# Hybrid encoder layer: local kernels of the state-space branch built on four 32-column strips, readout turns every second slot

## The reference

```python
def windowed_gqa_sink(q, k, v, sink):        # |t-s| <= 128, 8 heads, 2 kv heads, blocks of 128 queries
    scores = einsum(q, k) * HEAD_DIM ** -0.5 - slopes * dist      # + a sink logit per head
    probs = softmax(concat([scores, sink_logit]))[..., :-1]
    out = einsum(probs, v)

def s5_scan(u, lam, log_dt, b, c):           # per direction; 32 groups of 16 channels, 64 complex states
    lam_bar = exp(lam * dt);  b_bar = ((lam_bar - 1.0) / lam)[..., None] * b
    bu = einsum('blgc,gnc->blgn', u, b_bar)
    xs = associative_scan(lam_bar, bu)
    return einsum('blgn,gcn->blgc', xs, c).real

y = gelu(y_f + y_b + ssm_d * u)
```

## Time and profile before

| | us |
|---|---|
| median of 3 runs (2711.31 to 2716.84) | 2712.11 |
| the profiled execution, whole | 2706.54 |
| its span, first to last instruction | 2704.9 |
| granted clock of TensorE, mean over the span | 0.986 |
| attention stage in it, about | 258 to 477.9 |
| PE busy over the span | 2607.4 (96%) |
| DVE, ACT, POOL busy | 1597.7, 917.4, 827.5 |

### The profile page before, as it was taken

One profiled execution on the slowest core, in us unless ns is written; L12 is line 12 of the kernel. 1 busy time (PEld: TensorE's weight loads), 2 busy tenths in 40 slices (PEclk: granted clock), 3 DMA queues, 4 the chain that ended last, 5 costly groups with the idle time before them and its releaser, 6 DMA issues. The chain is left out here.

```text
span 2704.9 us, 33938 instructions
## 1 busy us (share of the span) xinstructions
PE 2607.4 (96%) x12118; PEld 2118.6 (78%) x12118; DVE 1597.7 (59%) x2050; ACT 917.4 (34%) x1579; POOL 827.5 (31%) x1070
## 2 busy tenths in 40 slices
PE   7999899999999799999999999999999999999997
PEld 6887566788887588878878888878888888887886
DVE  5202785687896274635687776697677762224342
ACT  5221776512211340123443333343333342123221
POOL 2072000387882000012244444434444320001111
PEclk9999999999999899999999999999999999999999
DMA  6484778644427636365434222212222264336653
GB/s 219 139 281 116 158 156 221 210 140 147 153 94 220 181 144 241 144 156 157 139 102 146 87 70 86 86 55 94 86 86 77 80 196 130 107 86 187 180 153 111
DMA packets 386110, 380.21 MB, mean 141 GB/s; under 512 B 52016, under 2 KB 322352, under 8 KB 381744
## 3 DMA queue, kind: packets, MB, share of 16 engines
q1 hardware_dynamic: 327024, 279.71, 35.7%
q10 hardware_dynamic: 49088, 50.91, 5.8%
q0 software_dynamic: 9856, 47.72, 5.2%
...
## 5 line engine op out<-in xcount | busy, mean ns | idle before, releaser
L522 PE MATMUL tl_banks<-gu_b_hi,gu_a_hi 128*128 128x512 f32 x1232 | 482.5, 392 | 13.4 <-DVE gu_b_lo L1760 8.0
L524 PE MATMUL tl_banks<-gu_b_lo,gu_a_hi 128*128 128x512 f32 x1232 | 481.5, 391 | 0.0
L523 PE MATMUL tl_banks<-gu_b_hi,gu_a_lo 128*128 128x512 f32 x1232 | 481.3, 391 | 0.0
L522 PEld LDWEIGHTS tl_banks<-gu_b_hi,gu_a_hi 128*128 128x128 f32 x1232 | 232.7, 189 | 65.0 <-issue 13.4
L146 PE MATMUL tl_banks<-dn_w_hi,dn_f_hi 128*128 128x512 f32 x704 | 274.3, 390 | 3.3 <-DVE dn_w_lo L1932 2.5
L147 PE MATMUL tl_banks<-dn_w_hi,dn_f_lo 128*128 128x512 f32 x704 | 273.9, 389 | 0.0
L148 PE MATMUL tl_banks<-dn_w_lo,dn_f_hi 128*128 128x512 f32 x704 | 273.9, 389 | 0.0
L523 PEld LDWEIGHTS tl_banks<-gu_b_hi,gu_a_lo 128*128 128x128 f32 x1232 | 232.7, 189 | 48.2
L524 PEld LDWEIGHTS tl_banks<-gu_b_lo,gu_a_hi 128*128 128x128 f32 x1232 | 232.4, 189 | 48.5
L1754 DVE TENSOR_TENSOR gu_a_lo<-gu_raw,gu_a_hi 128x512 fp32r<-128x512 f32 x220 | 198.3, 902 | 91.0 <-ACT gu_a_hi L1536 91.0
L1536 ACT ACTIVATE gu_a_hi<-gu_raw 128x512 fp32r<-128x512 f32 x220 | 138.4, 630 | 240.1 <-PE tl_banks L524 213.1
...
## 6 DMA issues: line engine op xcount, KB each, us to landing
...
```

What stands on the lines that cost most here:

```text
L522: pe.matmul(out, w_hi, x_hi, start=first, stop=False, skip_group_check=again)
L523: pe.matmul(out, w_lo, x_hi, start=False, stop=False, skip_group_check=again)
L524: return pe.matmul(out, w_hi, x_lo, start=False, stop=last, skip_group_check=again)
```

## The change

- A build now takes all four strips of 32 columns of the PE array: pair w = 4 j + part goes to the partitions 32 part to 32 part + 31 of `t_psum`. One bank then holds all 16 pairs of a direction. There are four builds instead of eight, each of 16 matmuls instead of 8 (the same 64 in all), two for each direction, at slots 75, 76, 107 and 108. DVE takes the bank away once for each direction, over 128 partitions.
- `kernels` has 128 partitions by 4 x 15 x 16 values instead of 32 by 16 x 15 x 16. `place_local` therefore needs 8 DMAs for each l instead of 2 (64 instead of 16, each a quarter of the size), `d_diag` is loaded by 8 DMAs instead of 2, and its mask takes three POOL additions instead of one.
- `add_diagonal` moves from slot 105 to 110.
- The readout turns move from slots 10, 11, 12, 13 to 10, 12, 14, 16; the turns of the input tables one slot later.
- `turn_share`, `copy_share`, `apply_share` and `store_out` move one slot later in every tile (2, 3, 5, 6 to 3, 4, 6, 7).
- The table code moves into two generators (`into_tables`, `outof_tables`) with a semaphore and a scratch tile for each direction; the 96 instructions stay on DVE in the same order.

```diff
@@ -2377,16 +2378,17 @@
               [outof[1][r][:].rearrange("p q k c -> p (q k c)")[:, 0:table] for r in range(2)]]
     b_table = [[b_flat[d][r].rearrange("p (q l c) -> p q l c", q=QS, l=SSM_L) for r in range(2)] for d in range(2)]
     params, bbar, rising, falling = bases.params, bases.bbar, bases.rising, bases.falling
-    late = m.sb("kernels", [P, QS * SPAN * SSM_CH])
-    kernels = carve(late, {"kernels": (2 * SSM_CH, (QS, SPAN, SSM_CH))})["kernels"]
+    PARTS = 4
+    late = m.sb("kernels", [P, 2 * 2 * 4 * 2 * SSM_N])
+    kernels = carve(late, {"kernels": (P, (QS // PARTS, SPAN, SSM_CH))})["kernels"]
 
     c_rows = carve(late, {"c_rows": (P, (2, 2, 4, 2 * SSM_N))})["c_rows"]
     c_t = m.sb("c_t", [P, 2, 2, QS, SSM_CH])
 
-    d_diag = m.sb("d_diag", [2 * SSM_CH, QS, SSM_CH])
-    d_mask = m.sb("d_mask", [2 * SSM_CH, SSM_CH])
+    d_diag = m.sb("d_diag", [P, QS // PARTS, SSM_CH])
+    d_mask = m.sb("d_mask", [P, 4 * SSM_CH])
     b_pair = m.sb("b_pair", [P, 2, 2, QS, 2, SSM_CH])
-    table_temp = m.sb("table_temp", [P, QS // 4, POWERS, SSM_CH])
+    table_temp = [m.sb(f"table_temp{d}", [P, QS // 4, POWERS, SSM_CH]) for d in range(2)]
 
     neg_scores = m.sb("neg_scores", [P, 2, WIDE])
     probs = m.sb("probs", [P, 2, WIDE])
...
-    PER_BANK = BANK // LC
-    K_BANKS = QS // PER_BANK
+    local_rows = local_scratch.rearrange("p (q a) m -> a p q m", a=2 * PARTS)
 
 
     COLUMNS = [slice(a * QS // 4, (a + 1) * QS // 4) for a in range(4)]
 
-    C_AT = {10 + n: n for n in range(4)}
-    INTO_AT = {**{25 + 2 * n: n for n in range(8)}, **{49 + 2 * n: 8 + n for n in range(8)}}
-    KERNELS_AT = {**{74 + 2 * n: n for n in range(K_BANKS)}, **{97 + 2 * n: K_BANKS + n for n in range(K_BANKS)}}
+    C_AT = {10 + 2 * n: n for n in range(4)}
+    INTO_AT = {**{26 + 2 * n: n for n in range(8)}, **{50 + 2 * n: 8 + n for n in range(8)}}
+    KERNELS_AT = {75: 0, 76: 1, 107: 2, 108: 3}
     PAIR_AT = {24 + n: n for n in range(8)}
-    DIAG_AT = 105
+    DIAG_AT = 110
 
     def keys_of(kind):
...
@@ -2508,10 +2546,10 @@
         def place_local(ls):
             sync.wait_ge(kernels_ready, 1)
             for l in ls:
-                for e in range(2):
-
-                    sync.dma_start(local_rows[l * SSM_CH:(l + 1) * SSM_CH, e],
-                                   kernels[e * SSM_CH:(e + 1) * SSM_CH, :, SSM_L - 1 - l:2 * SSM_L - 1 - l, :]
+                for a in range(2 * PARTS):
+
+                    sync.dma_start(local_rows[a, l * SSM_CH:(l + 1) * SSM_CH],
+                                   kernels[a * SSM_CH:(a + 1) * SSM_CH, :, SSM_L - 1 - l:2 * SSM_L - 1 - l, :]
                                    .rearrange("c q k o -> c q (k o)")).then_inc(local_placed, 16)
 
         load(1)
...
                     sync.dma_start(c_rows[:, d, r, :, twice * SSM_N:(twice + 1) * SSM_N], rows).then_inc(c_loaded, 16)
-        for e in range(2):
-            rows = ssm_d.rearrange("(a q e c) -> e a q c", a=1, e=2, c=SSM_CH)[e]
-            sync.dma_start(d_diag[e * SSM_CH:(e + 1) * SSM_CH], rows.broadcast_to([SSM_CH, QS, SSM_CH]))\
+        for e in range(2 * PARTS):
+            rows = ssm_d.rearrange("(a q e c) -> e a q c", a=1, e=2 * PARTS, c=SSM_CH)[e]
+            sync.dma_start(d_diag[e * SSM_CH:(e + 1) * SSM_CH], rows.broadcast_to([SSM_CH, QS // PARTS, SSM_CH]))\
                 .then_inc(d_loaded, 16)
         for n in range(2):
             load_u(n)
...
@@ -2535,19 +2573,23 @@
                 place_local(range(0, 2))
         place_local(range(2, SSM_L))
         sync.wait_ge(outof_stored, 4 * 16)
-        sync.wait_ge(local_placed, 2 * SSM_L * 16)
+        sync.wait_ge(local_placed, 2 * PARTS * SSM_L * 16)
...
         pool.wait_ge(bias_step, 2 + N_HEADS)
         pool.memset(b_pair[:], 0.0).then_inc(b_pair_zero, 1)
-        pool.wait_ge(d_loaded, 32)
-        pool.tensor_tensor(d_mask[:], ident[0:2 * SSM_CH, 0:SSM_CH], ident[0:2 * SSM_CH, SSM_CH:2 * SSM_CH],
-                           ALU.add).then_inc(d_diag_ready, 1)
-        pool.wait_ge(d_diag_ready, 1)
-        pool.tensor_tensor(d_diag[:], d_diag[:], d_mask[:].rearrange("p (a c) -> p a c", a=1)
-                           .broadcast_to([2 * SSM_CH, QS, SSM_CH]), ALU.mult).then_inc(d_diag_ready, 1)
+        pool.wait_ge(d_loaded, 2 * PARTS * 16)
+        for n, width in enumerate((64, 32, 16)):
+            of = d_mask if n else ident
+            if n:
+                pool.wait_ge(d_diag_ready, n)
+            pool.tensor_tensor(d_mask[:, 0:width], of[:, 0:width], of[:, width:2 * width], ALU.add)\
+                .then_inc(d_diag_ready, 1)
+        pool.wait_ge(d_diag_ready, 3)
+        pool.tensor_tensor(d_diag[:], d_diag[:], d_mask[:, 0:SSM_CH].rearrange("p (a c) -> p a c", a=1)
+                           .broadcast_to([P, QS // PARTS, SSM_CH]), ALU.mult).then_inc(d_diag_ready, 1)
         for b in range(TILES):
             pool.wait_ge(share_ready, b + 1)
...
@@ -2647,23 +2689,24 @@
             turn.then_inc(into_turned, 1)
 
         def make_kernels(n):
-            d, part = n // K_BANKS, n % K_BANKS
+            d, half = n // 2, n % 2
             k0 = 0 if d == 0 else 1
-            if part == 0:
+            if half == 0:
                 pe.wait_ge(outof_ready[d], 1)
-            if n:
-                pe.wait_ge(kernels_copied, n)
-            else:
-                pe.wait_ge(into_copied, 16)
-
-                pe.wait_ge(b_pair_ready, 8)
-            for j in range(PER_BANK):
-                w = part * PER_BANK + j
+                if d:
+                    pe.wait_ge(kernels_copied, 1)
+                else:
+                    pe.wait_ge(into_copied, 16)
+
+                    pe.wait_ge(b_pair_ready, 8)
+            for j in range(2 * half, 2 * half + 2):
                 for r in range(2):
-                    done = pe.matmul(t_psum[0:2 * SSM_CH, j * LC:(j + 1) * LC],
-                                     b_pair[:, d, r, w].rearrange("p e c -> p (e c)"),
-                                     outof[d][r][:, w, k0:k0 + SSM_L].rearrange("p k c -> p (k c)"),
-                                     start=r == 0, stop=r == 1)
+                    for part in range(PARTS):
+                        w = j * PARTS + part
+                        done = pe.matmul(t_psum[part * 2 * SSM_CH:(part + 1) * 2 * SSM_CH, j * LC:(j + 1) * LC],
+                                         b_pair[:, d, r, w].rearrange("p e c -> p (e c)"),
+                                         outof[d][r][:, w, k0:k0 + SSM_L].rearrange("p k c -> p (k c)"),
+                                         start=r == 0, stop=r == 1)
             done.then_inc(kernels_done, 1)
 
         pe.sem_inc(turned, 2)
...
@@ -2680,7 +2723,7 @@
                 turn_probs(b, i)
                 if i % QUAD and slot > QUAD:
                     weigh(slot // QUAD - 1, i % QUAD - 1)
-                if b and i == 2:
+                if b and i == 3:
                     turn_share(b - 1)
                 if slot in C_AT:
...
@@ -2773,23 +2779,23 @@
             dve.tensor_tensor(attn_t[:], attn_t[:], o_psum[:, b % 2], ALU.mult).then_inc(attn_ready, 1)
 
         def keep_kernels(n):
-            d, part = n // K_BANKS, n % K_BANKS
+            d, half = n // 2, n % 2
+            if half == 0:
+                return
             dve.wait_ge(kernels_done, n + 1)
-            mine = kernels[:, part * PER_BANK:(part + 1) * PER_BANK]
-            found = t_psum[0:2 * SSM_CH, :].rearrange("c (q k o) -> c q k o", q=PER_BANK, o=SSM_CH)
+            found = t_psum[:].rearrange("c (q k o) -> c q k o", q=QS // PARTS, o=SSM_CH)
             if d == 0:
-                dve.tensor_copy(mine[:, :, SSM_L - 1:SPAN], found).then_inc(kernels_copied, 1)
+                dve.tensor_copy(kernels[:, :, SSM_L - 1:SPAN], found).then_inc(kernels_copied, 1)
             else:
-                if part == 0:
-                    dve.wait_ge(kernels_copied, K_BANKS)
-                dve.tensor_tensor(mine[:, :, SSM_L - 1], mine[:, :, SSM_L - 1],
+                dve.wait_ge(kernels_copied, 1)
+                dve.tensor_tensor(kernels[:, :, SSM_L - 1], kernels[:, :, SSM_L - 1],
                                   found[:, :, SSM_L - 1], ALU.add).then_inc(kernels_added, 1)
-                dve.wait_ge(kernels_added, part + 1)
-                dve.tensor_copy(mine[:, :, 0:SSM_L - 1], found[:, :, 0:SSM_L - 1]).then_inc(kernels_copied, 1)
+                dve.tensor_copy(kernels[:, :, 0:SSM_L - 1], found[:, :, 0:SSM_L - 1]).then_inc(kernels_copied, 1)
 
         def add_diagonal():
-            dve.wait_ge(kernels_copied, 2 * K_BANKS)
-            dve.wait_ge(d_diag_ready, 2)
+            dve.wait_ge(kernels_added, 1)
+            dve.wait_ge(kernels_copied, 2)
+            dve.wait_ge(d_diag_ready, 4)
             dve.tensor_tensor(kernels[:, :, SSM_L - 1], kernels[:, :, SSM_L - 1], d_diag[:], ALU.add)\
                 .then_inc(kernels_ready, 1)
 
...
@@ -2803,7 +2809,7 @@
```

(8 more changed lines are left out.)

70 lines of the change are left out of this document (35 added, 35 removed).

## The result

| | before | after |
|---|---|---|
| median (range), 5 runs each | 2711.31 us (2710.34 to 2716.84) | 2729.48 us (2727.83 to 2733.02) |
| ratio | | 1.006, 95% interval 1.0046 to 1.0075 |
| profiled execution, span | 2704.9 | 2727.8 |
| next stage's first DMA on SP | 477.89 | 498.13 |
| the rest of the span behind it | 2227.0 | 2229.7 |

The account below looks back on a forecast made before the run. PE was taken to bound the attention stage until a load is missing, with tile 14 late behind outof in full queues. Terms -4.9 - 1.0 + 0 + 1.0 - 0.8 = -5.7 us gave 2706.4 us; range -8.5 to -3 us.

Parts of the forecast that it names:

- item 3: SP's 64 local DMAs: at a pitch of 0.47 us they land at 476.8 with the attention's end; 0 us.
- rival A: place_local: SP becomes the bound at 0.66 us a DMA, +12 us, kernel slower at 2718.4; chance 0.12.
- Item 1: Forward builds, slots 75 and 76: two packed builds of 1.3 us replace four of 1.87; -4.9 us.
- Rival B: Builds: the strips do not overlap, builds take 3.7 us, sum -0.9, 2711.2 us; chance 0.12.
- Item 2: Backward builds, slots 107 and 108: mostly hidden before PE's wait for tile 14, landing about 445; -1.0 us.
- Rival D: Tile 14 lands with its earlier issue, -4 there; with quicker small DMAs -8.7 in all, 2703.4; chance 0.06.
- Item 4: End of the stage: store_out of tile 14 one slot later delays the last store; +1.0 us, between 0 and 2.
- Item 5: Start of the stage: longer d_diag loads and POOL work against readout turns that wait less; -0.8 us, between -2.5 and +1.5.
- rival C: Start of the stage: clock falls after the wait for POOL, or tile 2 is late; +1.5, 2708.7 us; chance 0.14.

Follow-up runs that it names:

- e1: Changed kernel with the columns of local reordered in HBM, so each of the 64 DMAs writes rows of 2 KB: 2718.3 us, ratio 1.0024.
- e7: Changed kernel with 2 KB local rows, old slots except builds, d_diag loaded behind tile 3, half of outof stored behind tile 11's load: 2708.5 us.
- e8: Kernel of before with only outof of the first direction stored earlier, behind the load of tile 11: 2709.4 us, ratio 0.9987.
- e9: Kernel of before with only turn_share, copy_share, apply_share and store_out one slot later: 2716.5 us, ratio 1.0014.
- e10: Kernel of before with only INTO_AT, the turns of the input tables, one slot later: 2716.6 us, ratio 1.0012.
- e5: Kernel of before with all the slot shifts: readout turns two slots apart, input turns and share chain one slot later: 2718.9 us, ratio 1.0025.
- e2: Changed kernel with one 256 KB DMA per window of local instead of eight of 32 KB, and eight later loads instead of one: 2724.6 us.

## Why the prediction was wrong

The forecast was 2706.4, faster or the same; the time is 2729.5, outside the range. The step that failed first is the price in **item 3**: "the nearest rows are the stores of `y_ssm` ... a pitch of 0.47". Number of pieces and partitions were alike, and the `y_ssm` stores even move twice the bytes, 64 KB each. What set the price of these was whether a partition's data is one row on at least one side. The `local` stores, old and new, have short pieces on both sides; no `local` store seen had cost under 570 ns, as rival A said. Seen were 0.65 and 0.67 us a DMA. e1 shows the cause by giving them the plain side, and with it the 0.47.

Along SP the miss adds up. The last `local` DMA was to land at 476.8 and landed at 497.0, 20.2 us later: 9.4 for the last 48 (32.0 instead of 22.6), 3.0 for the first 16 (10.5 instead of 7.5), and 8.6 because `kernels_ready` let SP go at 447.8 instead of 439.2; the loads of tile 15 between them took 5.3, where 5.1 were forecast, and the last landed 1.4 us behind its issue instead of 2.4. Item 3 had also taken SP's start for granted ("`kernels_ready` comes from DVE in slot 110, near 439"), on a stage that would run ahead of before. It ran behind, for two reasons of other items.

**Item 1** was right on the mechanism and low on the size: 1.01 us for a build, not 1.3; masks 72 to 88 take 4.9 us less, just the forecast, though 7.5 - 2.0 = 5.5 us of PE went. Rival B is out.

**Item 2** was right as far as it went: the builds are hidden in a hole ahead of tile 14, forecast 6 us, seen 7.28. But it held the landing fixed at 445. `outof` was issued at 425.68 instead of 419.84, since SP stores it behind the load of tile 13, and that runs with the stage. Behind it one part of tile 14's load held SP for 6.38 us, where 3.03 were seen before, and tile 14 came at 453.5. e7 and e8 show that `outof` ahead of it is what it waits for. Rival D did not come.

**Item 4** expected 1.0 us at the end, 2 at most: the last store comes 8.1 us behind the last mask instead of 6.2, its upper bound; e9, with the share chain alone shifted, has 7.7, and e10 6.2. But its sentence "the shift by a slot keeps every distance between the engines and costs nothing" is false, by e9: 3.5 us, an interval from 0.01 to 0.27%. So, it seems, is "`INTO_AT` one slot later has slack at both ends: 0": 3.6 us by e10, whose interval still holds 0. Together, with the readout turns, they cost 7 us by e5, which is clear. Not all was shifted: the weighings, the turn of the values and the release of a tile's buffers stayed in their slots, and an ordered queue has more neighbours than those that a semaphore names.

**Item 5** had the signs of its terms, but not their sum. `d_diag` held SP for 5.0 us instead of 3.8, and the clause "if tile 2 ... does not hold slot 14" was the one that decided: tile 2 held it, for 7.3 us, and the granted clock fell at 284.4, one of the signs of rival C. Mask 16 came 3.4 us late, against a bound of +1.5. POOL was no cause; its four instructions took 0.34, 0.55 for two and 0.32 us, not 0.70 each, and PE waited for the first spread 1.72 us, 1.51 in before. Rival C was this mechanism at half its price.

**Rival A** (0.12) was what happened: 0.65 and 0.67 us a DMA, where it had said 0.66, and SP's last `local` DMA 9 us behind ACT's last store. It priced this at +12 against a stage otherwise on time. I gave it too little: rows of the very operation spoke for it, a look-alike against. The Trainium skill, DMA: Bandwidth & Descriptors, "Rules for kernel authors", advises to coalesce small transfers; by e2 that is right for the issuing engine (8 `local` DMAs of 256 KB end 29 us earlier on SP than 64 of 32 KB), and the layout and the eight loads that came with it cost part of it in the later stage.
